# Norm sums, RWKV operands and PV steps moved in a two-block kernel on one Trainium2 core

## The reference

```python
y = xf * lax.rsqrt(jnp.mean(jnp.square(xf), axis=-1, keepdims=True) + EPS)
...
return jnp.square(jax.nn.relu(h @ w_mlp1[l])) @ w_mlp2[l]
...
s = jnp.einsum("bqhd,bkhd->bhqk", qn, kn) + jnp.einsum("bqhr,bkr->bhqk", qr, kr)
p = jax.nn.softmax(s.astype(jnp.float32) * ATTN_SCALE, axis=-1).astype(v.dtype)
return jnp.einsum("bhqk,bkhd->bqhd", p, v)
```

```python
sa = jnp.einsum('bhvk,bhk->bhv', S, -kk_t)
S = (S * w_t[:, :, None, :]
     + sa[..., None] * (kk_t * a_t)[:, :, None, :]
     + v_t[..., None] * k_t[:, :, None, :])
return S, jnp.einsum('bhvk,bhk->bhv', S, r_t)
```

## Time and profile before

| | |
|---|---|
| three runs, us | 1926.4, 1926.8, 1927.97 (median 1926.8) |
| the profiled execution, us | 1930.27 |
| its span, us | 1928.5 |
| instructions | 25914 |
| TensorE busy | 1798.7 us (93%), 10452 matmuls |
| VectorE busy | 925.1 us (48%) |
| ScalarE busy | 400.0 us (21%) |
| GpSimd busy | 278.4 us (14%) |
| mean granted clock of TensorE | 0.969 |
| DMA, mean | 133 GB/s |

### The profile page before, as it was taken

One profiled execution on the slowest core, in us unless ns is written; L12 is line 12 of the kernel. 1 busy time (PEld: TensorE's weight loads), 2 busy tenths in 40 slices (PEclk: granted clock), 3 DMA queues, 4 the chain that ended last, 5 costly groups with the idle time before them and its releaser, 6 DMA issues.

```text
span 1928.5 us, 25914 instructions
## 1 busy us (share of the span) xinstructions
PE 1798.7 (93%) x10452; PEld 1406.9 (73%) x10452; DVE 925.1 (48%) x1738; ACT 400.0 (21%) x757; POOL 278.4 (14%) x292
## 2 busy tenths in 40 slices
PE   5999998999999998889999799999799899999997
PEld 1344444888888885568999688764598778788886
DVE  1375424646754446746875412378631342355511
ACT  3124442220122103452210012200412100300000
POOL 0002511220022110142320200155000000000000
PEclk8999999999999998999999899899999999999999
DMA  8653831123332222113544444232412244244443
GB/s 322 270 202 143 316 138 66 66 88 109 131 109 88 88 88 88 66 66 132 174 160 171 158 155 139 73 131 88 153 46 89 86 177 143 81 148 153 153 153 109
DMA packets 38416, 256.22 MB, mean 133 GB/s; under 512 B 4096, under 2 KB 7168, under 8 KB 8608
## 3 DMA queue, kind: packets, MB, share of 16 engines
q1 hardware_dynamic: 35808, 239.82, 35.1%
q0 software_dynamic: 1920, 10.62, 1.6%
q10 hardware_dynamic: 576, 4.19, 0.5%
HBM read 247.27 MB, written 7.34 MB: 132 GB/s over the span
## 4 chain that ended last, share of the span: by engine, by line
PE 81%; DVE 10%; ACT 2%; issue 2%; DMA 2%; POOL 1%; SPq 0%; ACTq 0%; DVEq 0%; POOLq 0%
PE ps L575 80%; DMA ring<-weights 1%; DVE arena L1835 1%; DVE arena L1991 1%; PE ps L739 1%; DMA cs_raw<-c_t 0%; POOL aux L1626 0%; DVE aux L1863 0%; DVE arena L1864 0%; POOL aux L1617 0%; DVE arena L1865 0%; ACT hT L1278 0%; DVE small L1874 0%; DVE ring L1906 0%; ACT aux L1351 0%
## 5 line engine op out<-in xcount | busy, mean ns | idle before, releaser
L575 PE MATMUL ps<-hT,ring 128*128 128x256 f32 (+3 forms) x3184 | 741.2, 392 | 24.5 <-issue 17.0
L575 PEld LDWEIGHTS ps<-hT,ring 128*128 128x128 f32 (+1 forms) x3184 | 576.0, 194 | 179.6 <-issue 105.1
L575 PE MATMUL ps<-arena,ring 128*128 128x256 f32 (+3 forms) x1756 | 351.8, 356 | 4.3 <-DVE arena L1865 3.2
L575 PEld LDWEIGHTS ps<-arena,ring 128*128 128x128 f32 (+1 forms) x1756 | 293.6, 190 | 52.8 <-issue 11.7
L575 PE MATMUL ps<-arena,sums 128*128 128x256 f32 (+1 forms) x768 | 136.5, 327 | 1.3 <-DVE aux L1929 1.3
L575 PEld LDWEIGHTS ps<-arena,sums 128*128 128x128 f32 x768 | 118.2, 191 | 12.3 <-DVE aux L1929 2.5
L1617 POOL TENSOR_TENSOR aux<-aux 128x256 f32<-128x256 f32 (+1 forms) x42 | 42.9, 1021 | 507.5 <-ACT aux L1233 506.9
L1233 ACT ACTIVATE aux<-xT 128x256 f32<-128x256 f32 (+1 forms) x64 | 31.0, 494 | 284.9 <-DVE xT L2021 93.3
L1626 POOL TENSOR_SCALAR aux<-aux,small 128x512 f32<-128x512 f32 (+1 forms) x48 | 70.8, 1483 | 123.1 <-DVE small L1881 122.7
L575 PE MATMUL ps<-hT,sums 128*128 128x128 f32 (+1 forms) x512 | 78.8, 302 | 0.4 <-DVE aux L1929 0.4
L575 PE MATMUL ps<-arena 64*64 64x64 f32 (+3 forms) x1392 | 66.6, 238 | 10.4 <-DVE arena L2161 9.1
(11 more groups left out here) (337 smaller groups left out, 1940.9 us busy)
## 6 DMA issues: line engine op xcount, KB each, us to landing
ring<-weights SPq DMA_DIRECT2D x224, 1024.0 KB, 4.9
kept_turns<-aux ACTq DMA_DIRECT2D x4, 1024.0 KB, 5.5
arena<-kept_turns POOLq DMA_DIRECT2D x6, 512.0 KB, 4.7
kept_keys_values<-arena POOLq DMA_DIRECT2D x1, 2048.0 KB, 7.4
arena<-kept_keys_values POOLq DMA_DIRECT2D x1, 2048.0 KB, 8.2
tab<-tables SPq DMA_DIRECT2D x1, 1426.5 KB, 11.0
xT<-ctx_t SPq DMA_DIRECT2D x1, 1024.0 KB, 6.0
xT<-x_t SPq DMA_DIRECT2D x1, 1024.0 KB, 8.2
```

What stands on the lines that cost most here:

```text
L575: ins = nc.tensor.matmul(o_, lhsT, rhs, start=start, stop=stop, skip_group_check=True)
```

## The change

Three things are done.

1. Norms 2 and 4 are summed by GpSimd over six tiles (`SUMMED`), and TensorE adds tiles 6 and 7 in two matmuls of their own. In layer 1 the adds stand before GpSimd's wait for the last bank, and so before the reload of the turn tables. The other norms stay as they are.
2. In the RWKV stage VectorE signals `r_at` and `r_kk` first, then `r_rt` and `r_kh`, then, after the masks of m1 and m1t, `r_a2` and `r_k2`. TensorE waits for each part where it needs it. Two gate tiles that stood between n2 and m2 and between a2t and k2t now stand before the first product.
3. PV of a pair is done one step later, and `probT` has four buffers.

```diff
+SUMMED = {1: 7, 2: 6, 3: 7, 4: 6, 6: 7, 7: 7, 8: 7}
-        probT = auxf[:, 2048:3584].rearrange("p (n t) -> p n t", n=3)
+        probT = auxf[:, 2048:4096].rearrange("p (n t) -> p n t", n=4)
...
             def norm_stat_step(key, norm, k, s, K=KD):
-                if norm and k < KD - 2:
+                n_sum = SUMMED[norm] if norm else 0
+                if norm and k < n_sum - 1:
                     return
-                first = 0 if norm == 0 else KD - 2
-                if k == first:
+                if k == 0 or (norm and k == n_sum - 1):
                     open_bank(key, "hold")
-                if norm and k == KD - 2:
+                if norm and k == n_sum - 1:
                     pe.wait_ge(S["square_sums"], SUM_ORDER.index(norm) + 1)
                     mm(bank(key)[:, s], ones, sq[:, 0, s], True, False)
                     return
-                pe.wait_ge(S["squares"], KD * norm + k + 1)
-                mm(bank(key)[:, s], ones, sq[:, k, s], k == first, k == K - 1, key if k == K - 1 else None)
+                pe.wait_ge(S["squares"], KD * norm + (2 * k + 2 if norm == 4 else k + 1))
+                mm(bank(key)[:, s], ones, sq[:, k, s], k == 0, k == K - 1, key if k == K - 1 else None)
...
-                stat_of_x(KD - 2)
-                stat_of_x(KD - 1)
+                for n in range(SUMMED[2 * l + 2] - 1, KD):
+                    stat_of_x(n)
...
-                for j in range(len(todo) + LAG + 1):
+                for j in range(len(todo) + LAG + 2):
...
-                    t = j - LAG - 1
+                    t = j - LAG - 2
...
+            gate_tiles(2)
             pe.wait_ge(S["rw_dve"], 5)
...
             product("m1t", r_at, r_kk)
+            pe.wait_ge(S["rw_dve"], 6)
             product("n1", r_at, r_rt)
             product("n2", r_kh, r_rt)
-            gate_tiles(1)
             product("m2", r_kh, r_kk)
+            pe.wait_ge(S["rw_dve"], 7)
             product("a2t", r_a2, None)
-            gate_tiles(1)
             product("k2t", r_k2, None)
...
             product("d2t", c_d, c_dt)
+            pe.wait_ge(S["rw_dve"], 9)
             product("qt", c_d2, c_qt, ("d2", "n1"))
...
-                for k in range(1, KD - 1):
+                for k in range(1, SUMMED[norm]):
                     pool.wait_ge(S["squares"], KD * norm + each * (k + 1))
...
-                if l == 0:
-                    square_sum(2, slice(0, 2 * T))
+                square_sum(2 * l + 2, slice(0, 2 * T), 1 + l)
...
             turns_back(0)
             turns_back(1)
-            square_sum(4, slice(0, 2 * T), 2)
...
             dve.wait_ge(S["rw_act"], 2)
+            did(tt(r_at[:, :, :], r_at[:, :, :], r_k2[:, :, :], ALU.mult))
+            dve.wait_ge(S["rw_act"], 3)
             did(v.tensor_copy(pend[:, :, :], r_rt[:, :, :].rearrange("p i (c t) -> p i c t", t=CHUNK)[:, :, :, CHUNK - 1]))
-            did(tt(r_at[:, :, :], r_at[:, :, :], r_k2[:, :, :], ALU.mult))
-            did(tt(r_kh[:, :, :], r_k[:, :, :], r_k2[:, :, :], ALU.mult))
+            did(tt(r_kk[:, :, :], r_kk[:, :, :], r_a2[:, :, :], ALU.mult), "rw_dve")
             did(tt(r_rt[:, :, :], r_rt[:, :, :], r_r[:, :, :], ALU.mult))
-            dve.wait_ge(S["rw_act"], 3)
-            did(tt(r_kk[:, :, :], r_kk[:, :, :], r_a2[:, :, :], ALU.mult))
-            for dst, src in ((r_a2, r_at), (r_k2, r_kh)):
-                for i in range(4):
-                    did(tt(dst[:, i, :].rearrange("p (c t) -> p c t", t=CHUNK), src[:, i, :].rearrange("p (c t) -> p c t", t=CHUNK),
-                           pend[:, i, :].unsqueeze(2).to_broadcast([P, NCH, CHUNK]), ALU.mult),
-                        "rw_dve" if dst is r_k2 and i == 3 else None)
+            did(tt(r_kh[:, :, :], r_k[:, :, :], r_k2[:, :, :], ALU.mult), "rw_dve")
...
                 masked(("m1t", half), b64(c_dt, half), "m_dt")
+            for dst, src in ((r_a2, r_at), (r_k2, r_kh)):
+                for i in range(4):
+                    did(tt(dst[:, i, :].rearrange("p (c t) -> p c t", t=CHUNK), src[:, i, :].rearrange("p (c t) -> p c t", t=CHUNK),
+                           pend[:, i, :].unsqueeze(2).to_broadcast([P, NCH, CHUNK]), ALU.mult),
+                        "rw_dve" if dst is r_k2 and i == 3 else None)
             for half in range(2):
                 masked(("n1", half), b64(r_n1, half), "m_le")
```

More of the change, by code:

```diff
@@ L762, in _ @@
                                 mm(o_[64 * hh:64 * hh + 64, qt * P:(qt + 1) * P], vtok[:, kt, h * DV:(h + 1) * DV],
-                                   probT[:, (t - 1 + hh) % 3, kt * P:(kt + 1) * P], kt == 0, end,
+                                   probT[:, (t - 1 + hh) % 4, kt * P:(kt + 1) * P], kt == 0, end,
                                    key if t % per == per - 1 and end and hh else None)
@@ L799, in _ @@
                 per = PAIRS1 // (2 if l == 0 else 1)
-                last_half = 1 if l == 0 else 0
                 def h_act(form, j, first, l=l):
@@ L830, in stat_of_x @@
                 def stat_of_x(n, l=l):
-                    if l == 0:
-                        norm_stat_step(("st", 2), 2, n, slice(0, 2 * T))
-                    else:
-                        if n < KD - 2:
-                            return
-                        if n == KD - 2:
-                            open_bank(("st", 4), "hold")
-                            pe.wait_ge(S["square_sums"], SUM_ORDER.index(4) + 1)
-                            mm(bank(("st", 4)), ones, sq[:, 0, :], True, False)
-                            return
-                        pe.wait_ge(S["squares"], KD * 4 + 2 * n + 2)
-                        mm(bank(("st", 4)), ones, sq[:, n, :], False, True, ("st", 4))
+                    norm_stat_step(("st", 2 * l + 2), 2 * l + 2, n, slice(0, 2 * T))
                 for what, hf, p, g, groups in mlp_order(l):
@@ L862, in _ @@
                                key if closes and j == 3 else None)
-                    if what == "m2" and hf == last_half and g == 0 and p:
-                        stat_of_x(2 * p - 2)
-                        stat_of_x(2 * p - 1)
-                stat_of_x(KD - 2)
-                stat_of_x(KD - 1)
+                for n in range(SUMMED[2 * l + 2] - 1, KD):
+                    stat_of_x(n)
             pools["run"].append(7)
@@ L1350, in _ @@
                         finished(act, ("t", l, t))
-                        did(f(probT[:, t % 3, 0:nk], bank(("t", l, t))[:, 0:nk], ACT.Copy), key=("t", l, t))
+                        did(f(probT[:, t % 4, 0:nk], bank(("t", l, t))[:, 0:nk], ACT.Copy), key=("t", l, t))
                         per = len(todo) // 4
@@ L1536, in product @@
                     copied((name, half), flat2(dst, half), n=512)
-            gates_(1)
+            gates_(2)
             product("a2t", r_a2t)
-            gates_(1)
             product("k2t", r_k2t)
@@ L1614, in square_sum @@
                 pool.wait_ge(S["squares"], KD * norm + each)
-                for k in range(1, KD - 1):
+                for k in range(1, SUMMED[norm]):
                     pool.wait_ge(S["squares"], KD * norm + each * (k + 1))
-                    did(nc.gpsimd.tensor_tensor(sq[:, 0, s], sq[:, 0, s], sq[:, k, s], ALU.add), "square_sums" if k == KD - 2 else None)
+                    did(nc.gpsimd.tensor_tensor(sq[:, 0, s], sq[:, 0, s], sq[:, k, s], ALU.add),
+                        "square_sums" if k == SUMMED[norm] - 1 else None)
             for l in range(LAYERS):
```

## The result

The changed kernel takes 1895.15 us (median of 4 runs, 1894.65 to 1895.81), the one before beside it 1926.6 (4 runs, 1923.38 to 1927.97): a ratio of 0.9834, 95% interval 0.9822 to 0.9847. I had forecast 1902.2 with a range of 1895.7 to 1909.0. The profiled execution of the changed kernel took 1894.65 us (span 1892.9), 35.6 less than the profiled one of before, which was itself a long one.

The account below looks back on a forecast made before the run. TensorE work was taken as the bound (81% of the span), so cuts count only where it idles or runs at lower clock. Five terms sum to 24.6 us off, giving 1902.2 us against the 1926.8 median, range 1895.7 to 1909.

Parts of the forecast that it names:

- Layer 0's norm: Norm after layer 0's MLP: an early matmul of the sum shortens the statistic by 2.7 us, bounds 1.8 to 3.3.
- Layer 1's norm: Norm after layer 1's MLP: adds moved ahead of the reloads save 7.8 us, bounds 6.7 to 9.4.
- The 0.66 for a blocking reload issue: Layer 1's norm: GpSimd's reload issue was taken to block VectorE's update; without blocking, the term is 0.66 us larger.
- RWKV: RWKV products: TensorE's 9.05 us wait for VectorE goes and the clock stays up; 9.8 us saved, bounds 7.3 to 10.7.
- PV in layer 1: Layer 1's attention: PV one step later removes waits for ScalarE's copy; 4.0 us saved, bounds 3.0 to 5.7.
- PV in layer 0: Layer 0's attention: an earlier TensorE waits for streamed weights instead; only 0.3 us saved, bounds -0.5 to 2.
- The sum: Whole kernel: five terms, 2.7 + 7.8 + 9.8 + 4.0 + 0.3, save 24.6 us.
- a rival at 0.12: Both norms after the MLPs: TensorE restarts at full clock, 5.3 us more saved, 1896.9 us; chance 0.12.
- The range: Whole kernel: 1895.7 to 1909 us, the bounds of the sum, with the first two rivals inside.
- a wait taking the place of the old one: Attention: scores, maximum, exponential and GpSimd's multiplication hold the loop, so 4.3 us stay; 1906.5 us, chance 0.08.
- VectorE taking over: RWKV products: waits for masks or half clock in narrow products return 7 us; 1909.2 us, chance 0.08.
- the slower case: RWKV onward: narrow products bring the clock down for good, costing 50 us; 1952.2 us, chance 0.02.

Follow-up runs that it names:

- e9: The changed kernel run again with no edit: 1893.58 us (1891.45 to 1898.29, 5 runs).
- e1: The kernel before with only PV one step later in both layers and four buffers of transposed probabilities: 1921.3 us, ratio 0.9956.
- e2: The kernel before with only PV one step later, in layer 0 alone: 1923.93 us, ratio 0.9980.
- e4: The kernel before with the RWKV part alone (three signals, two gate tiles moved): 1913.96 us, ratio 0.9925.
- e13: The kernel before with only the two gate tiles moved ahead of the RWKV wait, VectorE's single signal kept: 1918.05 us.
- e16: The kernel before with 11 of 12 modulation blocks in layer 0's attention multiplying constants in SBUF instead of streamed weights: 1922.76 us.

## Why the prediction was right and wrong

- *Layer 0's norm, 2.7:* 3.3. The clock held to the statistic's end, which was my upper bound. I had put its fall inside the statistic, as far behind TensorE's stop as before; it came only after 727.
- *Layer 1's norm, 7.8 (6.7 to 9.4):* 7.9, the size in part by luck, since two steps erred against each other. The 0.66 for a blocking reload issue was wrong: the update beside a reload took 0.48 us, beside an add 1.5 to 2.2. Against it, the last two matmuls took 3.41 us, near all at half clock (the clock's mean is 0.53 in the second from 1079), where I had taken the middle between half and full without a reason. The Trainium skill (SBUF — State Buffer, "Who interferes with whom") has a VectorE instruction with two SBUF inputs contend with a GpSimd instruction that reads SBUF, and infers that writing descriptors doesn't need what it holds; the trace agrees on both. The adds moved into the MLP cost nothing, as priced: TensorE's MLP is as long as before.
- *RWKV, 9.8:* 9.7, with the wait of 0.73 that I put at 0.9. This was the term with the longest working, and nearly every step of it held.
- *PV in layer 1, 4.0:* 3.1 in one execution, with a stretch of half clock in it, 4.3 in another. GpSimd took 1.6 us back, where my lower bound had one.
- *PV in layer 0, 0.3 (-0.5 to 2):* 2.8 without the stream, and 2.8 with it once the weight waits are taken off. This is the step that failed: "An earlier TensorE waits for weights instead." I read 80% busy DMA engines and 301 GB/s as a stream that sets the pace. The row doesn't show that: e9 moved 327 GB/s in the same stretch, at a share of 0.86. The wait rows spoke against it, since TensorE's three waits for the copy stood there as they do in layer 1, and they go in full if the stream isn't the limit.
- *The sum.* With 3 for layer 0 it would have been 27.3, and 1899.5, inside the range. The medians saved 31.5 and 32.5, another 4 to 5 us. That is the second step that failed: where the code is the same I put the clock at nothing, without a reason, and the stretch from layer 1's norm to RWKV is 3.7 us shorter with the norm edit. I had a rival at 0.12 (the clock holds behind the two statistics), and its price of 5.3 was near by luck: behind these two, where the next GEMM starts, the clock gave 0.8 us and took 0.3. Between the GLA part and 1330 the profiles of before, e1, e2, e4 and e13 have 31 to 34 us at half clock, all fourteen with the norm edit 20 to 24. But e16, without the norm edit, has 24 too. So what shortens these stretches, over 100 us behind any edit, stays open.
- *The range* ended where all terms are at their bounds. It had no term for the difference between one profiled execution and the next, which here is 5 us in one stage alone. The first exponential of layer 0's attention, ahead of every edit, stands anywhere from 175.5 to 179.1 us.
- Of the other rivals, a wait taking the place of the old one came only in layer 1's attention, with 1.6 of 5.7 us; VectorE taking over and the slower case didn't come: the clock reads 1.00 in the products.

## What to carry to other kernels

A busy DMA isn't a bound by its share: ask which wait ends last, and whether the landing moves when the consumer comes earlier. An order of work that lets TensorE run something useful through a wait keeps the clock as well, and one useful tile moved (6.7 us and more by the medians) was worth more than extra matmuls that only hold the clock. And before filling a break, look at what the filling itself needs: if its bank comes free only at the end of the break, it runs behind it. A term of a forecast that is read from one pair of executions should carry what a second pair would change, here 5 us in a stage of 77.

## What I had not expected of the hardware

The same code differs by 5 us in one stage (75.4 to 80.4) from execution to execution, with waits for the landing of weights of 1.6 to 8.0 us. A VectorE update with two SBUF inputs takes 0.48 us beside the issue of a DMA by GpSimd, and up to 2.23 beside GpSimd's add. And in code that the change doesn't touch the time at half clock went from 31 to 34 us down to 20 to 24.
